# Hybrid decoder layer, one core: gate and up projections of both FFNs by seven block products for eight, gated result kept in DRAM, down projection as a second phase

## The reference, cut to what matters

```python
D_MODEL = 1024
D_FF = 2816

def swiglu_ffn(x, g, w_gate, w_up, w_down):
    h = rmsnorm(x, g)
    return (jax.nn.silu(h @ w_gate) * (h @ w_up)) @ w_down

xp = xp + 0.5 * swiglu_ffn(xp, ffn1_norm[l], ffn1_w_gate[l], ffn1_w_up[l], ffn1_w_down[l])
```

## Time and profile before

| | before |
|---|---|
| median of 3 runs | 2710.73 us (2709.63 to 2711.07) |
| the profiled execution's own time | 2712.6 us |
| its span | 2710.8 us |
| PE busy | 2610.2 us (96%), 16950 matmuls |
| DVE busy | 1213.9 us (45%) |
| ACT busy | 607.0 us (22%) |
| POOL busy | 738.7 us (27%) |
| granted TensorE clock, mean | 0.977 of full |

### The profile page before, as it was taken

One profiled execution on the slowest core, in us unless ns is written; L12 is line 12 of the kernel. 1 busy time (PEld: TensorE's weight loads), 2 busy tenths in 40 slices (PEclk: granted clock), 3 DMA queues, 4 the chain that ended last, 5 costly groups with the idle time before them and its releaser, 6 DMA issues.

```text
span 2710.8 us, 43047 instructions
## 1 busy us (share of the span) xinstructions
PE 2610.2 (96%) x16950; PEld 2459.0 (91%) x16950; DVE 1213.9 (45%) x1785; ACT 607.0 (22%) x1240; POOL 738.7 (27%) x448
## 2 busy tenths in 40 slices
...
DMA packets 206319, 185.36 MB, mean 68 GB/s; under 512 B 8696, under 2 KB 192089, under 8 KB 203398
## 3 DMA queue, kind: packets, MB, share of 16 engines
...
## 4 chain that ended last, share of the span: by engine, by line
PE 92%; DVE 4%; ACT 1%; DMA 1%; issue 1%; ACTq 0%; DVEq 0%; SPq 0%
PE ps L366 24%; PE ps L365 24%; PE ps L362 24%; PE ps L1406 2%; PE ps L1432 2%; PE ps L1472 2%; PE ps L1418 1%; PE ps L1526 1%; PE ps L1598 1%; PE ps L1733 1%; PE ps L1596 1%; PE ps L1488 1%; PE ps L1713 1%; DMA ring<-in_cache_mem_k 1%; DVE acc_ffn L682 1%
## 5 line engine op out<-in xcount | busy, mean ns | idle before, releaser
L362 PE MATMUL ps<-h_hi,w_hi 128*128 128x352 f32 x2832 | 917.5, 324 | 27.7 <-DVEq L864 21.9
L365 PE MATMUL ps<-h_lo,w_hi 128*128 128x352 f32 x2832 | 916.8, 324 | 0.0
L366 PE MATMUL ps<-h_hi,w_lo 128*128 128x352 f32 x2832 | 916.3, 324 | 0.0
L1189 POOL CAST w_hi<-w_raw 128x1024 fp32r<-128x1024 f32 x192 | 201.8, 1051 | 1534.3 <-PE ps L362 681.3
L362 PEld LDWEIGHTS ps<-h_hi,w_hi 128*128 128x128 f32 x2832 | 534.0, 189 | 29.9 <-issue 27.4
L365 PEld LDWEIGHTS ps<-h_lo,w_hi 128*128 128x128 f32 x2832 | 533.7, 188 | 1.2
L366 PEld LDWEIGHTS ps<-h_hi,w_lo 128*128 128x128 f32 x2832 | 534.0, 189 | 0.0
L1195 POOL TENSOR_TENSOR w_lo<-w_raw,w_hi 128x1024 fp32r<-128x1024 f32 x192 | 471.7, 2457 | 15.4
L366 PE MATMUL ps<-g_hi,w_lo 128*128 128x352 f32 x1056 | 341.3, 323 | 0.0
L365 PE MATMUL ps<-g_lo,w_hi 128*128 128x352 f32 x1056 | 340.8, 323 | 0.0
L362 PE MATMUL ps<-g_hi,w_hi 128*128 128x352 f32 x1056 | 339.7, 322 | 0.3
...
## 6 DMA issues: line engine op xcount, KB each, us to landing
w_raw<-in_ffn_w_gate SPq DMA_DIRECT2D x44, 512.0 KB, 3.8
w_raw<-in_ffn_w_up SPq DMA_DIRECT2D x44, 512.0 KB, 3.8
...
ring<-in_cache_mem_k SPq DMA_DIRECT2D x16, 512.0 KB, 4.1
ring<-in_cache_mem_v SPq DMA_DIRECT2D x16, 512.0 KB, 4.6
w_raw<-in_w_in SPq DMA_DIRECT2D x14, 512.0 KB, 3.9
x_keep<-x_res SPq DMA_DIRECT2D x1, 4224.0 KB, 12.5
```

The source lines that it names most:

```text
L362: mm = pe.matmul(out, w_hi[:, slot, c0:c0 + m], hi, start=start, stop=False)
L365: pe.matmul(out, w_hi[:, slot, c0:c0 + m], lo, start=False, stop=False)
L366: return pe.matmul(out, w_lo[:, slot, c0:c0 + m], hi, start=False, stop=stop)
L1189: pool.tensor_copy(w_hi[:, s, 0:w], w_raw[:, s, 0:w]).then_inc(w_hi_done, 1)
```

## The change

The gate and up products are made two chunks at a time. For such a pair and one of the two projections (called a row in the code; 22 rows for an FFN, gate rows and up rows in turn), the weights are a block matrix of A11, A12, A21, A22 (2 chunks of features by 2 halves of the 8 planes), and the activations one of B11, B12, B21, B22 (2 halves of the planes by 2 halves of the tokens, 528 columns each). Seven products (steps 0 to 6) take the place of eight:

The diff, cut to what the prediction speaks of (empty lines left out):

```diff
-FF_GROUPS = (6, 5)
-FF_ROUNDS = FF_CHUNKS // sum(FF_GROUPS)
+FF_PAIRS = FF_CHUNKS // 2
+FF_ROWS = 2 * FF_PAIRS
+FF_GROUPS = (6, 5, 6, 5)
+TH = (SEQ + DEC_BATCH * DEC_SEQ) // 2
+TQ = TH // 2
...
+            def make(self, dve, t, k):
+                plane, half, other, op = {T1: (k, 0, y_keep[:, k, :], ALU.subtract),
+                                          T2: (k + HQ, 1, right_32[T1][:, k, :], ALU.add),
+                                          T3: (k + HQ, 1, y_keep[:, k, :], ALU.subtract),
+                                          T4: (k + HQ, 0, right_32[T2][:, k, :], ALU.subtract)}[t]
+                if t in (T1, T3):
+                    dve.wait_ge(*self.kept(k))
+                else:
+                    dve.wait_ge(*self.made(T1 if t == T2 else T2, k))
+                dve.scalar_tensor_tensor(out=right_32[t][:, k, :], in0=self.x(plane, half), scalar=self.gain(plane),
+                                         in1=other, op0=ALU.mult, op1=op).then_inc(self.s_made, 1)
...
+        FF_SLOTS = (0, 8, 0, 8)
+        PIECES = [(g, i) for g, n in enumerate(FF_GROUPS) for i in range(0, n, 2)]
+        STEPS = 7
+        COPIES, ADDS = 4, 8
+        BANKS = (0, 2, 4, 6, 0, 2, 4)
+        HOMES = (0, 1, 2, 3, 0, 1, 2)
...
+                def row(j, s):
+                    for half in range(2):
+                        src = (wgr, wur)[s][:, HQ * half:HQ * (half + 1), bass.ds(2 * P * j, 2 * P)]
+                        if isinstance(j, int) and first and j == 0 and s == 0:
+                            sp.dma_start(dst[half], src).then_inc(w_landed[half], 16)
+                        else:
+                            unit(self.u0 + 4 * j + 2 * s + half, half, dst[half], src)
...
+                row(0, 0)
+                row(0, 1)
+                with sp.Fori(1, FF_PAIRS) as j:
+                    row(j, 0)
+                    store(j - 1)
+                    row(j, 1)
+                last = FF_ROWS - 1
+                sp.wait_ge(self.g_stored, 16 * (self.op + FF_PAIRS - 1))
+                for i in range(3):
+                    sp.wait_ge(*self.steps_done(last, i))
+                    piece(i)
+                down(0, 0)
+                down(0, 1)
+                for i in range(3, 6):
+                    sp.wait_ge(*self.steps_done(last, i + 1))
+                    piece(i)
+                store(FF_PAIRS - 1)
+                for m in range(2, KC):
+                    down(0, m)
...
+                    for p in range(STEPS):
+                        if p < 5:
+                            pe.wait_ge(self.left_lo, 5 * rows + p + 1)
+                        else:
+                            pe.wait_ge(w_split, u + p - 4)
+                        b = BANKS[p]
+                        if p < 3 and first:
+                            if p == 0:
+                                for done, value in self.ready:
+                                    pe.wait_ge(done, value)
+                        elif p < 4:
+                            if not first:
+                                pe.wait_ge(*self.added(r - 1, (5, 6, 8, 8)[p]))
+                            if p == 3 and s == 1 and isinstance(j, int):
+                                pe.wait_ge(self.norm.s_rt, self.norm.ot + NTT)
+                        else:
+                            pe.wait_ge(*self.copied(r, (3, 4, 4)[p - 4]))
+                            pe.wait_ge(*self.added(r, (0, 1, 2)[p - 4])) if p > 4 else None
+                        for t in range(2):
+                            for k in range(HQ):
+                                if first and t == 0:
+                                    pe.wait_ge(*self.norm.lo_done(p, k))
+                                c = 512 * HOMES[p] + k * P
+                                mm = product(pe, ps[:, b + t, 0:TQ], c // 1024, c % 1024, P,
+                                             right_hi[p][:, k, t * TQ:(t + 1) * TQ], right_lo[p][:, k, t * TQ:(t + 1) * TQ],
+                                             k == 0, k == HQ - 1, p < 2 and t == 0 and k == 0)
+                            mm.then_inc(self.m_done, 1)
...
+            def left_free(self, eng, r, p):
+                if p >= 4:
+                    eng.wait_ge(*self.steps_done(r, p - 4))
+                elif r:
+                    eng.wait_ge(*self.steps_done(r - 1, (4, 5, 6, 3)[p]))
+                elif self.nth:
+                    eng.wait_ge(w_used, self.u0 + p // 2)
+            def raw_landed(self, eng, r, half):
+                eng.wait_ge(w_landed[half], 16 * (self.u0 // 2 + r + 1))
+            def left_highs(self, act, r, ps_of):
+                a11, a12, a21, a22 = raws()
+                made = 4 * (self.r0 + r)
+                for p in ps_of:
+                    if p in (0, 2, 6):
+                        self.raw_landed(act, r, 0 if p == 0 else 1)
+                        self.left_free(act, r, p)
+                        src = {0: a11, 2: a12, 6: a22}[p]
+                    else:
+                        act.wait_ge(self.left_made, made + {1: 1, 4: 2, 3: 3, 5: 4}[p])
+                        src = s2_keep[:, :, :] if p == 4 else left(w_lo32, p)
+                    if p == 4:
+                        self.left_free(act, r, p)
+                    act.activation(left(w_hi, p), src, ACT.Copy).then_inc(self.left_hi, 1)
+            def left_sides(self, pool, r):
+                a11, a12, a21, a22 = raws()
+                rows = self.r0 + r
+                made = 4 * rows
+                def make(out, x, y, op):
+                    pool.tensor_tensor(out, x, y, op).then_inc(self.left_made, 1)
+                def low(p, src):
+                    pool.wait_ge(self.left_hi, STEPS * rows + p + 1)
+                    ins = pool.tensor_tensor(left(w_lo, p), src, left(w_hi, p).bitcast(F32), ALU.subtract)
+                    if p < 5:
+                        ins.then_inc(self.left_lo, 1)
+                    else:
+                        ins.then_inc(w_split, 1)
+                self.raw_landed(pool, r, 0)
+                self.raw_landed(pool, r, 1)
+                self.left_free(pool, r, 1)
+                make(left(w_lo32, 1), a21, a22, ALU.add)
+                low(0, a11)
+                pool.wait_ge(self.left_made, made + 1)
+                if rows:
+                    pool.wait_ge(self.left_lo, 5 * rows)
+                make(s2_keep[:, :, :], left(w_lo32, 1), a11, ALU.subtract)
+                pool.wait_ge(self.left_made, made + 2)
+                low(1, left(w_lo32, 1))
+                low(2, a12)
+                self.left_free(pool, r, 3)
+                make(left(w_lo32, 3), a12, s2_keep[:, :, :], ALU.subtract)
+                pool.wait_ge(self.left_made, made + 3)
+                low(3, left(w_lo32, 3))
+                low(4, s2_keep[:, :, :])
+                self.left_free(pool, r, 5)
+                make(left(w_lo32, 5), a11, a21, ALU.subtract)
+                pool.wait_ge(self.left_made, made + 4)
+                low(5, left(w_lo32, 5))
+                low(6, a22)
...
+                def first_copies(r):
+                    act.wait_ge(*self.steps_done(r, 0))
+                    j, s = r // 2, r % 2
+                    if r == 0:
+                        act.wait_ge(*norm.made(T3, HQ - 1))
+                    elif r == 1:
+                        act.wait_ge(*norm.factors(2))
+                    elif s == 0:
+                        act.wait_ge(*self.muls(j))
+                    if s == 1 and self.op + j:
+                        act.wait_ge(self.g_stored, 16 * (self.op + j))
+                    for q in (0, 1, 2):
+                        act.activation(self.quarter(s, q), self.banks(0), ACT.Copy).then_inc(self.cp_done, 1)
+                def last_copy(r):
+                    act.wait_ge(*self.steps_done(r, 1))
+                    act.activation(self.quarter(r % 2, 3), self.banks(1), ACT.Copy, scale=-1.0).then_inc(self.cp_done, 1)
...
+                self.left_highs(act, 1, range(4))
+                norm.roots(act)
+                for r in range(1, FF_ROWS):
+                    first_copies(r)
+                    self.left_highs(act, r, (4,))
+                    last_copy(r)
+                    self.left_highs(act, r, (5, 6))
+                    if r == FF_ROWS - 1:
+                        g_high(0)
+                        g_high(1)
+                    if r % 2:
+                        silus(r // 2)
+                    if r < FF_ROWS - 1:
+                        self.left_highs(act, r + 1, range(4))
+                for c in range(2, FF_CHUNKS):
+                    g_high(c)
...
+                p, q, copies = ((1, 1, 4), (2, 0, 4), (3, 1, 4), (4, 1, 4), (4, 2, 4), (5, 2, 4), (None, 3, 4), (6, 2, 4))[n]
+                out = self.quarter(r % 2, q)
+                if p is not None:
+                    dve.wait_ge(*self.steps_done(r, p))
+                if n == 0:
+                    dve.wait_ge(*self.copied(r, copies))
+                if n in (2, 3, 5, 6, 7):
```

(29 more changed lines are left out.)

581 lines of the change are left out of this document (372 added, 209 removed).

## The result

The changed kernel takes 2761.1 us (median of 4 runs, 2758.8 to 2766.1) where the kernel before, on the same chip, takes 2710.9: a ratio of 1.0185, 95% interval 1.0172 to 1.0198. It is slower by 1.9%, clear of the noise. The forecast was 2720 us and slower by 0.3%: the side is right, the size is 41 us short. The measured time lies inside the whole range (2672 to 2775), but outside the 2708 to 2744 of rival A, which was the forecast.

A forecast was written before the change was run, and what follows sets the result against it. PE's stream bounds the old kernel; in the new one POOL's chain, loads and the DVE-POOL lock hold the pair. -36.8 + 1.9 + 14.1 + 25.4 + 4.2 = +8.8 us gives 2720 us, range 2672 to 2775.

The forecast's parts named there:

- rival A: The forecast itself: POOL's chain, the load and the lock hold a pair at 43.7 to 45.5 us; 2708 to 2744 us; chance 0.50.
- the borders: First pairs of FFN1 (+2 us) and FFN2 (+14), both passages from products to down (+25), third down unit's weights (+4).
- the steady pairs: Twenty pairs, all but the first of each FFN: 44.3 us each, 1.84 less than before, -37 us.
- rival C: Load-POOL-load loop worse: loads 4.5 us, lock 3 us a row, a pair 47 us, 2774 us in all; chance 0.16.
- the lock: DVE and POOL exclude each other on shared SBUF ports: 1.25 us after a gate row, 2.65 us after an up row.
- So both loops stand at 20.3 us and neither has slack: Per row: POOL's chain plus weight load, and PE's loop (m1 waits for step 5, step 0 for l0), both 20.3 us.
- PE's own row: Matmuls of 264 columns cost 0.120 us each, a step of 24 2.88 us, a row 20.2 us, a pair 40.4 us.
- Rival B: PE sets the pace: DVE slips between POOL's instructions, loads land in 3.4 us, a pair 41.5 us, 2664 us; chance 0.17.
- FFN1's first pair: PE begins at about 42 us instead of 55.4, then waits for DVE; the next row begins at 106.5 us: +2 us.
- FFN2's first pair: After w_co PE waits for the right sides and the roots; the next row begins 61.4 us after w_co: +14 us.
- To the down phase: PE waits for DVE's low parts of g, 10.7 us idle and about 2 us of lower clock, twice: +25 us.
- Group 1's third unit: Six chunks loaded ahead of the third down unit's weights, ready after 16.5 us where two units last 14.4: +4 us, both FFNs.

The follow-up runs named there:

- e7: Changed kernel with slot 0 loaded after m4, m4 ahead of l4, l6 ahead of l5, m1 waiting for step 4 instead of 5, m2 ahead of l0: pair 42.67 us.
- e1: Changed kernel, but SP may load slot 0 of the next row once m4 is done, not after l5: 23 to 27 us faster, pair 45.04 us.
- e11: Changed kernel with early loads, l0 ahead of m1 and DVE's scalings by rs cut to 32 of 1056 columns: 16.7 us faster than without that cut, pair 40.9 us.
- e12: Changed kernel with early loads, l0 ahead of m1, and low parts of chunks 2 to 5 made ahead of scalings in the last up row: 2657.1 us.
- e13: e12, and in FFN1 ACT makes hi0 and hi1 ahead of the second token half's copies and B22's high parts: 2657.6 us against e12's 2657.1.

## Why the prediction was right on the side and short in size

The side was close to even by the prediction's own chances (slower 0.51). It came out because the borders cost what was forecast and a little more, while the saving in the steady pairs, which was to pay for most of them, did not come. That 2761 us lies in the whole range is owed to rival C, whose 2774 is nearer than A's 2720.

**The steady pairs (forecast -37 us, measured -1).** The failing step is "A load of this shape lands in 3.4 us; the second of two close together is held up ... I take 3.7", with 0.3 us for the hand-overs: 4.0 us between l6 and m1. Its own rows 12 had 4.2 and 5.4 us for two such loads. The two loads of a row are issued 1.2 us apart and m1 comes 4.7 to 5.5 us after l6 (4.99 and 5.05 in the rows above): 2 us more a pair, which is the whole of 46.09 - 44.3 = 1.8. With slot 0 issued 2.6 to 3.3 us ahead of slot 1 the gap is 3.9 to 4.2 us (e7), and with 3.4 us it is 4.0 to 4.4 (e1). So the 4.0 of the forecast is right for a load whose forerunner is out of the way, and about 0.9 us of hold-up by the first load was missing. The rest of the timetable held: POOL's waits for ACT are 0.81 to 1.10 us at l3, 0.35 to 0.66 at l4 and 0.81 at l5 (0.8 each in the laid-out row), the lock 1.29 us after a gate row (m1 0.26, m2 1.03; forecast 1.25) and 2.4 after an up row (l0 0.5, m2 1.0, l1 0.9; forecast 2.65). The pair of 46.09 us lies between rival A (45.5 at most) and C (47); of C the part on the loads was right, that on the lock (3 us a row, measured 1.9) was not.

**"So both loops stand at 20.3 us and neither has slack"** was right for the home's loop and was used too little. With the lock the loop through step 5's home is 22.5 us a row, the load's 23.05. The prediction put all delays on one chain, 22.15 us a row with the lock, and took no other price for the second loop. The runs price it: it stands at 45.04 us a pair, so even with a load as forecast the pair would have been 45.0 and not 44.3 (15 us of the 37).

**PE's own row.** Forecast 0.120 us at 264 columns; twelve take 1.47 us, 0.1225. That is PE's bound of 40.9 to 41.2 us a pair, seen bare in e11. Rival B needed DVE to slip between POOL's instructions and loads of 3.4 us; neither came.

**FFN1's first pair (forecast +2, measured about +7).** Row 2 begins at 112.03 us instead of 106.5. "PE begins at about 42 us, when ACT has come to hi0" failed: ACT had it at 43.3, but l0 ended only at 50.3. That did not cost the time, however, since row 1 begins at 81 us wherever the first product stands (e12, e13). The step that did is DVE's sum ("at 0.62 us ... 0.3 to 1 us of waiting each"): DVE is busy nearly without a pause from 38 to 83 us, and four low parts took 2.6 to 6.9 us there instead of 2.5. Row 0's products end some 7 us later than the 70.5 of the forecast. Which of DVE's and POOL's meetings costs how much was not taken apart.

**FFN2's first pair (+14, measured +15).** w_co ends at 1945.5, row 0's products end 30.0 us later (31.5 forecast), row 1 begins after 32.1, and row 2 begins at 2008.23, 62.7 us after w_co (61.4).

**To the down phase (+25, measured +25).** The sum is right by luck, for its parts are not: PE's idle time is 8.3 and 7.7 us instead of 10.7 each, and the lower clock costs more. PE is busy 19.8 us for the 94 matmuls between 572 and 600 us, which at 0.160 each are 15.0. So the clock costs 4.7 us instead of 2, and 4.4 in FFN2. Of the idle time 2.3 us each were a wait for POOL's split, where the prediction had only waits for DVE. **Group 1's third unit** cost 1.3 + 2.0 us (+4 forecast).

Together: -1 + 7 + 15 + 25 + 3 = 49 us, and the spans differ by 48.5. Of the signs named in advance, the idle time before step 0 came (1.1 to 1.4 us). Less before step 1 came in up rows only (0.44 us); in gate rows it was the same 1.3 us. The long instructions were mostly POOL's (2.31 us), while of DVE's six of 1056 columns a pair only one reached 2.2 us. PE's idle time at the down phase came, but shorter than 10 to 13 us. The period, POOL's share (32 us busy of 46, for 28 of 44) and the first product did not come.
